# Two feed-forwards of a transformer kernel: their first chunk works on x without the root of the RMS norm, and its results are multiplied by the roots

## The chip, the cores and the metric

The kernel runs on one core of one Trainium2 chip, as one launch. The metric is the device time of that launch in microseconds (us). A core has a matrix engine (TensorE, PE in the profile), a vector engine (VectorE, DVE), a scalar engine (ScalarE, ACT), a general engine (GpSimd, POOL) and a queue for transfers (SyncE, SP). Each engine runs its own list of instructions in order; semaphores hold them together.

## The reference, cut to what matters

The reference is a model of two blocks of mixers, cross attentions and SwiGLU feed-forwards, and then a second part with a feed-forward of another kind. The change touches the two SwiGLU feed-forwards (l = 0 and 1) alone, each of which follows the output projection of a cross attention:

```python
def rms_norm(x, g, eps=NORM_EPS):
    xf = x.astype(jnp.float32)
    y = xf * lax.rsqrt(jnp.mean(xf * xf, axis=-1, keepdims=True) + eps)
    return (y * g.astype(jnp.float32)).astype(x.dtype)

def memory_cross_attention(h, mem, ..., wo):
    ...
    return out @ wo                       # 512 x 512 by 512 x 1024

def swiglu_ffn(h, norm, w13, w2):         # h 512 x 1024, hidden 2816
    u = rms_norm(h, norm) @ w13
    return (jax.nn.silu(u[..., :FFN_HIDDEN]) * u[..., FFN_HIDDEN:]) @ w2

h = h + memory_cross_attention(h, mem, ...)
h = h + swiglu_ffn(h, ffn_norm[i], ffn_w13[i], ffn_w2[i])
```

The root of a row (a token) is one number for all 1024 of its features, so (x * root * gain) @ W is (x * gain) @ W times that root, column by column of the tokens.

## The kernel before, in words

x lies transposed in SBUF: eight tiles `X[:, t, :]` of 128 features by 512 tokens. A product in nearly full float32 is made of three matmuls on float32r halves: weights high by x high, weights low by x high, weights high by x low (`Stream.tensor`). A `Stream` is a row of jobs, a job has chunks of up to 512 weight columns (four PSUM banks of 128 columns by 512 tokens), a chunk has one slice for each 128 features of the input. A slice is 12 matmuls for four banks. Chunks take the two sets of four banks in turn.

What each engine has to do for slices: ACT copies the weights of a slice to the high half (`round_slice`, L383), POOL subtracts to get the low half (`rest_of_slice`, L387), and there are four slots, so ACT's copy of slice s + 4 waits until PE is through slice s. All other work of ACT and DVE is written as generators, one for each finished chunk. `Stream.walk` puts them in a list and takes two steps of the first one in the list behind each slice (`rate` 2); on ACT these steps stand between the weight copies. DVE has no weight copies, so its instructions are simply the generators one after another, in the order of the chunks. A finish with `flush = 0` has ACT and DVE write out all that is pending at its first slice.

Around the change the stream of `cross_attention` has these jobs: `xo` (four slices in each of three chunks of 512, 256 and 256 columns; it adds to x), `up0` (six chunks of eight slices), `down0`, `up1`, `down1`.

- `AddToX.vector` (L853) adds each bank of `xo` to x. `AddToX.scalar` squares each tile of x (L628), `Rms.fold` (L635) adds up the squares of tiles 0 to 5 on DVE. `AddToX.tensor_end` stands at the end of `xo` in PE's list: a sum over the partitions of the folded squares and of tiles 6 and 7 (L649), idle matmuls that keep PE busy (`keep_busy`, L219), `spread_roots` (L657), and idle matmuls again.
- `Rms.roots` makes the mean (L695), ACT the square root (L663), DVE the inverse root (L2161 to L2169). `spread_roots` puts the roots in a PSUM bank, the same 512 in each partition. `Rms.scale` (L711) multiplies x by gain and by that bank, `Rms.round` (ACT, L669) makes the high half, `Rms.rest` (DVE, L678) the low half. PE waits for both in `up0`'s first chunk (`Finish.ready`, `ready_low`).
- `Gated` is the finish of `up0`: ACT takes the sigmoid of banks 0 and 1 (L1840), DVE multiplies by the same banks (L1852) and by banks 2 and 3 (L1857), ACT and DVE make the halves of the result (L1845, L1861).
- `Rider` is work of the second part that rides along: with each chunk of `up0`, DVE makes a sum over eight tiles of 128 by 512 (`Rider.vector`, one L905 and seven L910), behind the gated products of the chunk in DVE's list. In chunk c + 1, behind the slice t = 5, PE's list has `Gated.multiply(c)`: it waits for `made` of chunk c and, in `Rider.multiply`, for the rider's `summed` (four transposes, L930). `Rider.scalar` stands in ACT's list behind the gated work of the chunk; it waits for `first_used` and `summed` before it issues the next loads.

Of the kernel before, what the change touches and what calls it, by code (L numbers as in the profile page):

```python
# [286 lines left out]
class Stream:  # L287
# [53 lines left out]
    def tensor(self, pe):  # L341
        k = self.k
        for part in self.opening:
            part.tensor(pe)
        k.keep_busy(pe, 7, self.idle_first)
        for s, (q, job, c, t, finish, hi, lo) in enumerate(self.slices):
            if s >= self.opened:
                pe.wait_ge(self.rounded, s - self.opened + 1)
            finish.ready(pe, c, t)
            if t == 0 and q >= 2:  # L350
# [3 lines left out]
            for i, (w, a) in enumerate(((whi, hi(t)), (wlo, hi(t)), (whi, lo(t)))):  # L354
# [121 lines left out]
class Finish:  # L476

    flush, rate, after = None, 2, None  # L480

    def of(self, stream, job):
        self.stream, self.job = stream, job

    def signals(self, st):
        self.freed = st.signals(1)

    def ready(self, pe, c, t):

        if self.after and c == 0:  # L490
            self.after.await_high(pe, t)

    def ready_low(self, pe, c, t):
        if self.after and c == 0:
            self.after.await_half(pe, t)
# [85 lines left out]
class Rms:  # L581
# [122 lines left out]

    def scale(self, dve):

        for t in range(self.T + 1):
            if t < self.T:
                if self.split and t >= self.n_tmp:
                    dve.wait_ge(self.halved, self.tiles(t - self.n_tmp + 1))  # L710
                dve.scalar_tensor_tensor(out=self.tmp(t % self.n_tmp), in0=self.src(t), scalar=self.gain(t), in1=self.rows,  # L711
                                         op0=ALU.mult, op1=ALU.mult).then_inc(self.scaled, 1)
            if t >= 1 and self.split:
# [6 lines left out]
    def await_half(self, eng, t):  # L720
        eng.wait_ge(self.halved, self.tiles(t + 1))


# [58 lines left out]
class AddToX(Finish):  # L782
# [7 lines left out]
    def __init__(self, k, rms=None, gate=None, after=None, flush=None, ahead=None, rider=None, rms_later=False):  # L790
        self.folded = rms.T if rms_later else self.FOLDED
        if rms:
# [12 lines left out]
    def await_free(self, eng, c):  # L805
        eng.wait_ge(self.added, self.first(c + 1))
        if self.rms and not self.rms_later and c == len(self.job.widths) - 1:
            eng.wait_ge(self.rms.scaled, self.rms.T)
        if self.rider and c == 0:
# [12 lines left out]
    def tensor_end(self, pe):  # L822
        if self.rms_later:
            self.rms.sums_bank = self.sums_bank()
        elif self.rms:
            q2 = self.stream.first_chunk(self.job) + 2
# [21 lines left out]
    def vector(self, dve, link, q, c):  # L848
        for j in range(self.job.tiles(c)):
# [7 lines left out]
            ins.then_inc(self.added, 1)  # L857
            yield
        if self.rms:
            for t in range(max(self.first(c), 1), min(self.first(c + 1), self.folded)):  # L860
# [934 lines left out]
class Gated(Finish):  # L1795
# [8 lines left out]
    def signals(self, st):  # L1804
        self.bent, self.gated, self.made, self.rounded, self.halved = st.signals(5)
        if self.rider0 == 0:
            self.rider.signals(st)
# [17 lines left out]

    def tensor(self, pe, c, t):
        if c >= 1 and t == self.job.KT - 3:
            self.multiply(pe, c - 1)
# [6 lines left out]
    def scalar(self, act, q, c):  # L1835
        for p in range(2):
            self.stream.await_tile(act, q, p)
# [10 lines left out]

    def vector(self, dve, link, q, c):
        for p in range(2):  # L1850
# [7 lines left out]
        yield  # L1858
        for p in range(2):
            dve.wait_ge(self.rounded, 2 * c + p + 1)  # L1860
# [82 lines left out]
class Mixed(Finish):  # L1943
# [6 lines left out]
    def signals(self, st):  # L1950
        self.begun, self.tapped, self.bent, self.made = st.signals(4)

    def tensor_end(self, pe):
# [8 lines left out]
    def scalar(self, act, q, c):  # L1962
        for j in range(4):
            n = 4 * c + j
            self.stream.await_tile(act, q, j)
            at = self.tile0 + n
            act.activation(self.xbc[:, at, :], self.stream.bank(q, j), ACT.Identity, bias=col(self.k, "ssm_conv_b", at),  # L1967
                           scale=col(self.k, "ssm_conv_w3", at)).then_inc(self.begun, 1)
# [11 lines left out]

    def vector(self, dve, link, q, c):
        for lag in range(1, 4):
            for j in range(4):
                n = 4 * c + j
                if lag == 1:
                    dve.wait_ge(self.begun, n + 1)
                at = self.tile0 + n
                v = self.xbc[:, at, lag:S]
                ins = dve.scalar_tensor_tensor(out=v, in0=self.stream.bank(q, j)[:, 0:S - lag],  # L1989
                                               scalar=col(self.k, f"ssm_conv_w{3 - lag}", at), in1=v, op0=ALU.mult,  # L1990
# [751 lines left out]
def cross_attention(k, plan, l, name, out_halves, opening, squares_at, rows_at, spare_at, halves_at, mem_at, mem_halves_at,  # L2742
# [29 lines left out]

    rms = x_norm(k, lambda t: col(k, f"ffn_norm{l}", t), split_tiles(k, A_WORK, A_H), at=HID_AT + 8 * S)
    if l == 0:
# [32 lines left out]

def x_norm(k, gain, halves, shift=None, at=SCRATCH_AT, dst=None, n_squares=4):

# [3 lines left out]
    else:  # L2813
        tmp, n_tmp = (lambda i: dst[:, i, :]), DT
    return Rms(k, DT, lambda t: k.X[:, t, :], gain, halves, at, n_squares, at + n_squares * S, tmp, n_tmp, D, shift=shift)

# [1991 lines left out]
```

## Time and profile before

| | |
|---|---|
| median of 3 runs | 3426.64 us (3426.32 to 3426.74) |
| the profiled execution | 3427.0 us, its span 3425.3 us |
| PE busy | 3339.0 us, 97% of the span |
| DVE, ACT, POOL busy | 52%, 42%, 43% |
| mean granted clock of PE | 0.996 of full speed |

The trace gives for each instruction its engine, its line, start and duration. A matmul's duration is longer than its share of PE's time, since matmuls are pipelined; the pace is read from the distance of starts, or from the time and count of a long row. The two places of the change are at 545 us (l = 0) and at 1454 us (l = 1).

### The profile page before, as it was taken

What the parts mean: (1) busy time and instruction counts of PE and PEld (TensorE: products, weight loads), DVE (VectorE), ACT (ScalarE), POOL (GpSimd) and SP (SyncE); (2) the same over time, 40 slices, a digit from 0 to 9 for tenths busy, and PEclk for the clock granted to TensorE, in tenths of its full rate; (3) what the DMA queues carried; (4) which work ended last, traced back from release to release, by engine and by line L of the source; (5) the groups of instructions that cost most, each with busy time, mean ns of one, the idle gap of its engine ahead of it and who ended that gap; (6) DMA issues with size and microseconds to landing.
All of it is one profiled execution on the core that took longest, in us unless ns stands there. A gap on an engine that the chain in (4) does not pass through costs nothing. (4 is left out here: it accounts for less than half of the span.)

```text
span 3425.3 us, 48805 instructions
## 1 busy us (share of the span) xinstructions
PE 3339.0 (97%) x19319; PEld 2750.9 (80%) x19319; DVE 1781.4 (52%) x3104; ACT 1431.0 (42%) x2870; POOL 1483.4 (43%) x1337
## 2 busy tenths in 40 slices
PE   8999999999999999999999999999999999999999
PEld 7768778888877687888888877888888877888887
DVE  4665574636457674665363286445153176545243
ACT  4562354323344554532323246344343245444343
POOL 3330154454443545444544434445544433445543
PEclk9999999999999999999999999999999999999999
DMA  4210024545221022345443220222323220123321
GB/s 117 79 51 8 27 87 136 197 148 169 98 92 50 28 96 87 111 136 183 160 148 107 88 68 20 74 87 92 105 83 102 84 82 30 50 86 99 99 93 56
DMA packets 232830, 317.83 MB, mean 93 GB/s; under 512 B 9909, under 2 KB 149148, under 8 KB 232604
## 3 DMA queue, kind: packets, MB, share of 16 engines
q1 hardware_dynamic: 203206, 261.55, 23.8%
q10 hardware_dynamic: 29398, 53.17, 4.6%
q8 instruction: 154, 2.52, 0.3%
q14 instruction: 72, 0.59, 0.1%
HBM read 312.59 MB, written 2.10 MB: 92 GB/s over the span
## 5 line engine op out<-in xcount | busy, mean ns | idle before, releaser
L364 PE MATMUL banks<-split,split 128*128 128x512 f32 (+2 forms) x11760 | 2684.2, 389 | 27.7 <-ACT split L383 13.6
L364 PEld LDWEIGHTS banks<-split,split 128*128 128x128 f32 x11760 | 2186.9, 188 | 501.4 <-ACT split L383 24.4
L387 POOL TENSOR_TENSOR split<-kept,split 128x512 fp32r<-128x512 f32 (+2 forms) x1158 | 1356.4, 1176 | 1617.6 <-ACT split L383 1615.0
L383 ACT ACTIVATE split<-kept 128x512 fp32r<-128x512 f32 (+2 forms) x1158 | 646.1, 564 | 1460.1 <-PE banks L364 1416.8
L1913 DVE SCALAR_TENSOR_TENSOR work<-banks,kept,work 128x511 f32<-128x511 f32 (+1 forms) x176 | 120.4, 745 | 257.1 <-ACT work L1895 256.3
L910 DVE SCALAR_TENSOR_TENSOR work<-work,kept 128x512 f32<-128x512 f32 x168 | 195.5, 1164 | 6.0
L855 DVE SCALAR_TENSOR_TENSOR kept<-banks,kept 128x512 f32<-128x512 f32 x48 | 33.3, 745 | 209.6 <-PE banks L364 209.6
L853 DVE TENSOR_TENSOR kept<-banks,kept 128x512 f32<-128x512 f32 x64 | 40.5, 684 | 195.0 <-PE banks L364 195.0
L540 DVE COPY work<-banks 128x512 f32<-128x512 f32 (+1 forms) x64 | 37.4, 643 | 195.2 <-PE banks L364 195.2
L1852 DVE TENSOR_TENSOR work<-work,banks 128x512 f32<-128x512 f32 x44 | 28.3, 684 | 165.7 <-ACT work L1840 165.7
L1539 ACT ACTIVATE work<-work 128x128 f32<-128x128 f32 (+3 forms) x160 | 89.5, 560 | 48.4 <-DVE work L1599 47.6
L219 PE MATMUL banks<-kept 128*128 128x128 f32 x538 | 68.1, 277 | 10.7 <-PEq L246 10.7
L1989 DVE SCALAR_TENSOR_TENSOR work<-banks,kept,work 128x511 f32<-128x511 f32 (+2 forms) x72 | 49.1, 744 | 55.4 <-ACT work L1967 54.9
L219 PEld LDWEIGHTS banks<-kept 128*128 128x128 f32 x538 | 63.6, 192 | 13.7 <-issue 13.5
L1466 PE MATMUL banks<-kept,work 128*128 128x128 f32 x400 | 71.3, 276 | 0.6 <-ACT work L1539 0.6
L1599 DVE CUSTOM_DVE_ANT_0 work<-banks,kept 128x128 f32<-128x128 f32 (+3 forms) x96 | 46.8, 488 | 41.7 <-PE banks L1754 21.1
L635 DVE TENSOR_TENSOR work<-work 128x512 f32<-128x512 f32 x66 | 61.9, 938 | 5.4 <-DVE work L635 0.5
L1482 PE MATMUL banks<-work 128*64 128x128 f32 x592 | 61.3, 284 | 0.8 <-DVE work L1610 0.5
L669 ACT ACTIVATE split<-work 128x512 fp32r<-128x512 f32 x61 | 38.1, 630 | 56.0 <-DVE work L711 42.6
L1466 PEld LDWEIGHTS banks<-kept,work 128*128 128x128 f32 x400 | 48.8, 141 | 15.0 <-issue 6.2
L1895 ACT ACTIVATE work<-banks,kept 128x512 f32<-128x512 f32 x88 | 60.9, 771 | 0.0
L3693 PE MATMUL banks<-kept 64*64 64x64 f32 (+1 forms) x1408 | 55.4, 233 | 1.9 <-DVE kept L3928 1.4
(445 smaller groups left out, 3172.5 us busy)
## 6 DMA issues: line engine op xcount, KB each, us to landing
work<-in_mod_w ACTq DMA_DIRECT2D x48, 1024.0 KB, 5.9
kept<-in_ffn_w SPq DMA_DIRECT2D x94, 512.0 KB, 4.8
kept<-in_w_up SPq DMA_DIRECT2D x88, 512.0 KB, 4.5
kept<-in_w_in SPq DMA_DIRECT2D x36, 1024.0 KB, 5.0
kept<-in_od_w_in SPq DMA_DIRECT2D x20, 1024.0 KB, 5.0
kept<-in_ffn_w SPq DMA_DIRECT2D x18, 1024.0 KB, 5.2
kept<-in_w_down SPq DMA_DIRECT2D x18, 1024.0 KB, 5.0
kept<-in_ev_w_in SPq DMA_DIRECT2D x8, 1024.0 KB, 5.2
```

The lines of the kernel that those rows point to most:

```text
L219: pe.matmul(self.PS[:, bank, 0:P], self.ident, self.ones, start=True, stop=True)
L364: m = pe.matmul(self.bank(q, j), lhs, rhs, start=t == 0 and i == 0, stop=t == job.KT - 1 and i == 2)
L383: act.activation(self.weights(s, 0), self.source(s), ACT.Copy).then_inc(self.rounded, 1)
L387: pool.tensor_tensor(self.weights(s, 1), self.source(s), self.weights(s, 0), ALU.subtract).then_inc(self.k.slices_split, 1)
L635: dve.tensor_tensor(total, total, self.square_at(t), ALU.add).then_inc(self.folded, 1)
L910: ins = dve.scalar_tensor_tensor(out=self.sum, in0=self.slot[:, t, :], scalar=self.x[:, t:t + 1], in1=self.sum, op0=ALU.mult, op1=ALU.add)
L1466: m = pe.transpose(self.bank(self.TB[u % 2])[:, c * P:(c + 1) * P], self.prob[u % 4][:, c * P:(c + 1) * P], self.k.ident)
L1482: ins = pe.matmul(self.o_bank(h // 2)[i * 64:i * 64 + 64, t * P:(t + 1) * P], self.heads[h + i].v(c), self.probT[(u + i) % 3][:, c * P:(c ...
L1539: act.activation(tile, tile, ACT.Exp, bias=self.top[:, u % 8:u % 8 + 1], scale=-1.0, accum_out=self.total[:, u % 16:u % 16 + 1]).then_inc( ...
L1895: act.activation(self.cv[:, j, :], self.stream.bank(q, j), ACT.Identity, bias=col(self.k, f"conv_b_2{self.l}", at), scale=col(self.k, f"co ...
L1913: return dve.scalar_tensor_tensor(out=v, in0=self.stream.bank(q, j)[:, 0:S - lag], scalar=col(self.k, f"conv_w_2{self.l}{2 - lag}", self.c ...
L3693: m = pe.matmul(PS[half, bank, q * P:q * P + n], lhs(q)[half], rhs(q)[half], start=start, stop=stop)
```

## The change

For the norm in front of the two feed-forwards the class `Rms` gives way to `RmsBeside`.

- In `xo`, each tile of x gets its halves of x times gain, without the root, as soon as it is added: ACT makes the high half behind the square (`first_round`), DVE the low half behind the adds of the chunk (`first_rest`). All eight squares are folded on DVE (six before).
- `tensor_end` of `xo` issues nothing. `up0`'s first chunk takes the new halves (`await_first_high`, `await_first_half`), and no longer flushes. The sum stands behind its slice 2 (`SUM`), `spread_roots` behind its slice 4 (`SPREAD`), without idle matmuls.
- ACT's `root_of` stands behind the weight copy that waits for slice 3, and ACT copies the spread roots from PSUM to SBUF (`factors`, signal `kept`) behind the copy that waits for slice 5.
- `scale`, `round` and `rest` make the normed halves for chunks 1 to 5 in the same place as the first halves; `round` waits until PE is through the slice of chunk 0. `scale` reads the roots from SBUF (`factors`). On ACT these steps come two behind each weight copy.
- The first chunk's results take more steps on DVE (`first_products`): banks 0 and 1 times `factors`, times the sigmoid, times banks 2 and 3, times `factors`. They stand behind `scale` and `rest` in DVE's list, and in front of the rider's first sum.

```diff
 class Gated:
     def tensor(self, pe, c, t):
+        if self.early and c == 0:
+            self.early.beside(pe, t)
         if c >= 1 and t == self.job.KT - 3:
             self.multiply(pe, c - 1)
...
     def scalar(self, act, q, c):
         for p in range(2):
+            if self.early and c == 0:
+                act.wait_ge(self.first_made, p + 1)
+                act.activation(self.slot(1, p), self.slot(0, p), ACT.Sigmoid).then_inc(self.bent, 1)
+                continue
             self.stream.await_tile(act, q, p)
             if c >= 2:
                 act.wait_ge(self.halved, 2 * (c - 2) + p + 1)
+            elif self.early:
+                act.wait_ge(self.gated, p + 1)
...
+    def first_products(self, dve, q):
+        factors = self.early.factors
+        dve.wait_ge(self.early.kept, 1)
+        for p in range(2):
+            self.stream.await_tile(dve, q, p)
+            dve.tensor_tensor(self.slot(0, p), self.stream.bank(q, p), factors, ALU.mult).then_inc(self.first_made, 1)
+        yield
+        for p in range(2):
+            dve.wait_ge(self.bent, p + 1)
+            dve.tensor_tensor(self.slot(0, p), self.slot(0, p), self.slot(1, p), ALU.mult).then_inc(self.gated, 1)
+        yield
+        for p in range(2):
+            self.stream.await_tile(dve, q, 2 + p)
+            dve.wait_ge(self.gated, p + 1)
+            dve.tensor_tensor(self.slot(0, p), self.slot(0, p), self.stream.bank(q, 2 + p), ALU.mult).then_inc(self.second_made, 1)
+        yield
+        for p in range(2):
+            dve.wait_ge(self.second_made, p + 1)
+            dve.tensor_tensor(self.slot(0, p), self.slot(0, p), factors, ALU.mult).then_inc(self.made, 1)
+        yield
...
+class RmsBeside(Rms):
+
+    SUM, SPREAD = 2, 4
...
+    @property
+    def factors(self):
+        return self.sq[:, 3, :]
+
+    def first_round(self, act, t):
+        act.activation(self.first_halves(t)[0], self.src(t), ACT.Identity, scale=self.gain(t)).then_inc(self.first_rounded, 1)
+
+    def first_rest(self, dve, t):
+        dve.wait_ge(self.first_rounded, t + 1)
+        high, low = self.first_halves(t)
+        dve.scalar_tensor_tensor(out=low, in0=self.src(t), scalar=self.gain(t), in1=high, op0=ALU.mult,
+                                 op1=ALU.subtract).then_inc(self.first_halved, 1)
...
+    def beside(self, pe, t):
+        if t == self.SUM:
+            self.sum_folded(pe, self.k.PS[:, self.bank0 + 2, :])
+        if t == self.SPREAD:
+            self.spread_roots(pe, self.k.PS[:, self.bank0 + 3, :])
+
+    def finish_scalar(self, act, steps=1):
+        for _ in range(2 * self.SUM + 2):
+            yield
+        self.root_of(act)
+        for _ in range(2 * (self.SPREAD - self.SUM)):
+            yield
+        act.wait_ge(self.spread, 1)
+        act.activation(self.factors, self.rows, ACT.Copy).then_inc(self.kept, 1)
+        yield
+        for t in range(self.T):
+            if not self.first:
+                self.stream.await_slice(act, self.slice0 + t)
+            self.round(act, t)
+            yield
+
+
+    def finish_vector(self, dve, link):
+        self.roots(dve, link)
+        yield
+        dve.wait_ge(self.kept, 1)
+        yield from self.scale(dve, self.factors, self.first)
...
 class AddToX(Finish):
@@ scalar
                 self.rms.square(act, self.first(c) + j)
+            if self.beside:
+                self.rms.first_round(act, self.first(c) + j)
             yield
@@ vector
+        if self.beside:
+            for j in range(self.job.tiles(c)):
+                self.rms.first_rest(dve, self.first(c) + j)
+                yield
         if self.rms:
             for t in range(max(self.first(c), 1), min(self.first(c + 1), self.folded)):
                 self.rms.fold(dve, t)
@@ ffn_jobs
-    up0 = Gated(k, *hid, SG_AT, rider, 0, after=rms, flush=0)
+    up0 = Gated(k, *hid, SG_AT, rider, 0)
+    up0.early = rms
```

## Rows read from the trace of the kernel before

**Rows 1.** The page: span, busy time, the granted clock in 40 slices

```profile
span 3425.3 us, 48805 instructions
PE 3339.0 (97%) x19319; PEld 2750.9 (80%) x19319; DVE 1781.4 (52%) x3104; ACT 1431.0 (42%) x2870; POOL 1483.4 (43%) x1337
```

**Rows 2.** Timeline, l = 0: start us, us, engine, line, operation [idle before <-releaser]

```profile
544.62 1.08 PEld L649 LDWEIGHTS banks<-kept,work 128*128 128x128 f32 x8
...
544.84 1.05 PE L649 MATMUL banks<-kept,work 128*128 128x128 f32 x8
...
546.79 1.28 ACT L663 ACT_TABLE_LOAD   x1
...
548.53 0.20 ACT L663 ACTIVATE work<-work 128x4 f32<-128x4 f32 x1 [0.46 <-DVE work L695]
...
549.59 1.16 PE L657 MATMUL banks<-kept,work 128*128 128x128 f32 x8
...
550.79 1.41 DVE L711 SCALAR_TENSOR_TENSOR work<-kept,banks 128x512 f32<-128x512 f32 x2 [1.25 <-PE banks L657]
...
552.27 29.81 PEld L364 LDWEIGHTS banks<-split,split 128*128 128x128 f32 x132
```

**Rows 3.** Timeline, l = 1: the same two ends

```profile
1454.14 1.08 PEld L649 LDWEIGHTS banks<-kept,work 128*128 128x128 f32 x8
...
1461.79 30.27 PEld L364 LDWEIGHTS banks<-split,split 128*128 128x128 f32 x134
```

**Rows 4.** Timeline, l = 0: the rider's first sum and PE's transposes behind it

```profile
580.75 1.52 DVE L905 TENSOR_SCALAR work<-work,kept 128x512 f32<-128x512 f32 x1
...
582.31 8.28 DVE L910 SCALAR_TENSOR_TENSOR work<-work,kept 128x512 f32<-128x512 f32 x7
...
590.71 0.42 PEld L930 LDWEIGHTS banks<-kept,work 128*128 128x128 f32 x4 [0.47 <-issue]
...
591.10 21.62 PEld L364 LDWEIGHTS banks<-split,split 128*128 128x128 f32 x96
```

**Rows 5.** Timeline, l = 0, in xo: adds, squares, weight copies

```profile
533.48 2.48 DVE L853 TENSOR_TENSOR kept<-banks,kept 128x512 f32<-128x512 f32 x4 [11.51 <-PE banks L364]
...
534.49 1.14 ACT L628 ACTIVATE work<-kept 128x512 f32<-128x512 f32 x2
...
535.88 2.97 DVE L635 TENSOR_TENSOR work<-work 128x512 f32<-128x512 f32 x3
...
539.38 1.29 DVE L853 TENSOR_TENSOR kept<-banks,kept 128x512 f32<-128x512 f32 x2 [0.52 <-PE banks L364]
...
541.23 0.62 ACT L383 ACTIVATE split<-kept 128x512 fp32r<-128x512 f32 x1
```

**Rows 6.** Timeline, l = 0: two weight copies behind two slices, one split on POOL

```profile
571.66 0.63 ACT L383 ACTIVATE split<-kept 128x512 fp32r<-128x512 f32 x1 [2.09 <-PE banks L364]
...
574.38 0.63 ACT L383 ACTIVATE split<-kept 128x512 fp32r<-128x512 f32 x1 [2.09 <-PE banks L364]
...
575.09 1.29 POOL L387 TENSOR_TENSOR split<-kept,split 128x512 fp32r<-128x512 f32 x1 [1.43 <-ACT split L383]
```

**Rows 7.** Groups of DVE with shapes, 545 to 592 us: busy us, mean ns | idle before

```profile
L711 DVE SCALAR_TENSOR_TENSOR work<-kept,banks 128x512 f32<-128x512 f32 x8 | 5.8, 742 | 1.3 <-PE banks L657 1.3
L678 DVE TENSOR_TENSOR split<-work,split 128x512 fp32r<-128x512 f32 x8 | 5.5, 686 | 0.1
...
L1852 DVE TENSOR_TENSOR work<-work,banks 128x512 f32<-128x512 f32 x2 | 1.3, 684 | 15.7 <-ACT work L1840 15.7
L1857 DVE TENSOR_TENSOR work<-work,banks 128x512 f32<-128x512 f32 x2 | 1.3, 678 | 0.0
```

**Rows 8.** L910 over the whole trace: shortest, median, longest ns

```profile
L910 DVE SCALAR_TENSOR_TENSOR work<-work,kept x168: 750/753/1860, 582.3 to 1786.4; 128x512 f32<-128x512 f32 x168
```

**Rows 9.** Groups of DVE with shapes, 552 to 1000 us

```profile
L910 DVE SCALAR_TENSOR_TENSOR work<-work,kept 128x512 f32<-128x512 f32 x84 | 97.8, 1164 | 3.0
L1861 DVE TENSOR_TENSOR split<-work,split 128x512 fp32r<-128x512 f32 x22 | 21.0, 992 | 3.5 <-ACT split L1845 3.4
```

**Rows 10.** Timeline of PE: two restarts after long waits

```profile
138.49 11.21 PE L364 MATMUL banks<-split,split 128*128 128x512 f32 x36 [5.76 <-ACT split L383]
...
978.88 13.34 PE L364 MATMUL banks<-split,split 128*32 128x512 f32 x47 [4.64 <-ACT split L383]
```

**Rows 11.** Stretches: PE, PEld, DVE, ACT, POOL busy (x), granted clock, DMA share, GB/s

```profile
552.20:574.20 22.00, 22.00 (x100) 18.21 (x100) 8.95 (x14) 8.53 (x15) 8.91 (x7) 1.00 0.16 48
...
974.00:979.00 5.00, 0.36 (x3) 0.12 (x1) 4.96 (x8) 2.81 (x6) 0.10 (x1) 0.83 0.00 0
979.00:985.00 6.00, 6.00 (x16) 4.27 (x17) 5.93 (x7) 2.02 (x4) 5.87 (x5) 0.58 0.54 178
```

More of the change, by code:

```diff
@@ L349, in tensor @@
             finish.ready(pe, c, t)
+            high, low = finish.early.first_halves(t) if finish.early and c == 0 else (hi(t), lo(t))
             if t == 0 and q >= 2:
@@ L353, in tensor @@
             n = job.tiles(c)
-            for i, (w, a) in enumerate(((whi, hi(t)), (wlo, hi(t)), (whi, lo(t)))):
+            for i, (w, a) in enumerate(((whi, high), (wlo, high), (whi, low))):
                 if i == 1:
@@ L476 @@
 class Finish:
-    flush, rate, after = None, 2, None
+    flush, rate, after, early = None, 2, None, None
     def of(self, stream, job):
         self.stream, self.job = stream, job
+        if self.early:
+            self.early.follow_with(stream, job)
     def signals(self, st):
@@ L703, in finish_vector, with scale @@
         yield from self.scale(dve)
-    def scale(self, dve):
+    def scale(self, dve, rows=None, first=None):
+        rows = self.rows if rows is None else rows
         for t in range(self.T + 1):
@@ L710, in scale @@
                     dve.wait_ge(self.halved, self.tiles(t - self.n_tmp + 1))
-                dve.scalar_tensor_tensor(out=self.tmp(t % self.n_tmp), in0=self.src(t), scalar=self.gain(t), in1=self.rows,
-                                         op0=ALU.mult, op1=ALU.mult).then_inc(self.scaled, 1)
+                if first:
+                    self.stream.await_slice(dve, self.slice0 + t)
+                dve.scalar_tensor_tensor(out=self.tmp(t % self.n_tmp), in0=self.src(t), scalar=self.gain(t), in1=rows, op0=ALU.mult,
+                                         op1=ALU.mult).then_inc(self.scaled, 1)
             if t >= 1 and self.split:
@@ L721, in await_half, with first_halves, signals, follow_with @@
         eng.wait_ge(self.halved, self.tiles(t + 1))
+class RmsBeside(Rms):
+    SUM, SPREAD = 2, 4
+    first = None
+    def first_halves(self, t):
+        hi, lo = self.first or (self.hi, self.lo)
+        return hi(t), lo(t)
+    def signals(self, st):
+        super().signals(st)
+        self.first_rounded, self.first_halved, self.kept = st.signals(3)
+    def follow_with(self, stream, job):
+        self.stream = stream
+        self.slice0 = next(s for s, piece in enumerate(stream.slices) if piece[1] is job)
+        self.bank0 = (stream.first_chunk(job) - 1) % 2 * 4
+    @property
[8 more added lines that the diff above has]
+                                 op1=ALU.subtract).then_inc(self.first_halved, 1)
+    def await_first_high(self, eng, t):
+        eng.wait_ge(self.first_rounded, t + 1)
+    def await_first_half(self, eng, t):
+        eng.wait_ge(self.first_halved, t + 1)
+    def beside(self, pe, t):
[22 more added lines that the diff above has]
+        yield from self.scale(dve, self.factors, self.first)
 class RowsLater(Rms):
@@ L807, in await_free @@
         if self.rms and not self.rms_later and c == len(self.job.widths) - 1:
-            eng.wait_ge(self.rms.scaled, self.rms.T)
+            if self.beside:
+                eng.wait_ge(self.rms.kept, 1)
+            else:
+                eng.wait_ge(self.rms.scaled, self.rms.T)
         if self.rider and c == 0:
@@ L824, in tensor_end @@
             self.rms.sums_bank = self.sums_bank()
-        elif self.rms:
+        elif self.rms and not self.beside:
             q2 = self.stream.first_chunk(self.job) + 2
@@ L1826, in tensor @@
     def tensor(self, pe, c, t):
+        if self.early and c == 0:
+            self.early.beside(pe, t)
         if c >= 1 and t == self.job.KT - 3:
@@ L1858, in vector @@
         yield
+    def vector(self, dve, link, q, c):
+        yield from self.first_products(dve, q) if self.early and c == 0 else self.products(dve, q, c)
         for p in range(2):
@@ L1951, in signals, with tensor, raw @@
         self.begun, self.tapped, self.bent, self.made = st.signals(4)
+        if self.early:
+            self.first_made = st.signals(1)
+    def tensor(self, pe, c, t):
+        if self.early and c == 0:
+            self.early.beside(pe, t)
+    def raw(self, q, c, j):
+        return self.sg[:, j, :] if self.early and c == 0 else self.stream.bank(q, j)
     def tensor_end(self, pe):
@@ L1981, in vector @@
     def vector(self, dve, link, q, c):
+        if self.early and c == 0:
+            dve.wait_ge(self.early.kept, 1)
+            for j in range(4):
+                self.stream.await_tile(dve, q, j)
+                dve.tensor_tensor(self.raw(q, c, j), self.stream.bank(q, j), self.early.factors, ALU.mult).then_inc(
+                    self.first_made, 1)
+                if j % 2:
+                    yield
         for lag in range(1, 4):
```

34 lines of the change are left out of this document (24 added, 10 removed).

## The prediction

> **What bounds the kernel now.** Read first the busy line of the page: PE works 97% of the span [rows 1]. So a change can only win by taking waits or idle matmuls out of PE's list, and anything that makes PE wait is paid in full, unless PE waits further on for something that goes on meanwhile. Then the timeline at the change-over from `xo` to `up0`. PE's sum (L649) begins at 544.62, the first slice of `up0` at 552.27: 7.65 us in which PE does 3 us of sums and spreading and otherwise idle matmuls [rows 2]. At l = 1 it is again 7.65 us [rows 3]. These two stretches, 15.3 us or 0.45% of the span, are all that the change can win.
>
> Last, one looks for the next place behind the change where PE meets work of the engines that the change loads. It is the rider. Its first sum ends at 582.31 + 8.28 = 590.59, and PE's transposes, which wait for it, begin at 590.71, after 0.47 us without work [rows 4]. So PE and DVE arrive there together, 8 + 6 slices behind the start of `up0`: 552.27 to 590.24, or 2.71 us a slice; the distance of ACT's copies says the same, 574.38 - 571.66 = 2.72 [rows 6]. The cover of that sum is used up already.
>
> **The change part by part**, in times of l = 0.
>
> *When up0 starts.* ACT gets a high half of about 0.6 us behind each square, DVE a low half of about 0.75 (the shortest L910, which has the same two inputs in SBUF [rows 8]) behind each add. The adds of chunk 0 end at 535.96; ACT's squares begin at 534.49 [rows 5]. ACT has eight steps of 0.6 us and a weight copy between, so its fourth high half is there at 539.7. DVE's fourth low half is then done at 540.4, its three folds, 2.97 us before the change [rows 5], at 543.1 (I take 2.7, between that and three times the 0.75 above), and the adds of tiles 4 and 5, so far at 539.38 [rows 5], come at 543.1 to 544.4. ACT waits for them with squares and high halves, 4 x 0.6 us, and only then stands the copy of `up0`'s first weights, so far at 541.23 [rows 5]. It ends at 546.9. PE starts there, not at 544.6: of the 7.65 us, 5.4 are won. Bounds: 544.7 if all this hides, 548.5 if each DVE operation takes the mean of the stretch with POOL at work, 1.16 and 0.99 us [rows 9]. A further 0.4 us go as PE waits for POOL's first low half (1.29 us [rows 6], against 0.9 us for the four matmuls in front).
>
> *What stands inline.* The sum costs PE 1.05 us and spreading 1.16 [rows 2]. PE is through slice 2 at 546.9 + 0.4 + 3 x 2.71 = 555.4, through slice 3 at 555.4 + 1.05 + 2.71 = 559.2, through slice 4 at 561.9. The root is late by 0.4: ACT's copy behind slice 3 ends at 559.9, the table load takes 1.28 (so far it lay under the sum), the root 0.2, and from the root's start to the spreading it is 549.59 - 548.53 = 1.06 [rows 2]: 562.3. So PE is ready for the transposes at 546.9 + 0.4 + 1.05 + 0.4 + 1.16 + 37.97 = 587.9, which is 2.3 us earlier than the 590.24 of before.
>
> *When the rider's sum is there.* ACT copies the roots behind the copy that waits for slice 5: PE leaves that slice at 561.9 + 0.4 + 1.16 + 2.71 = 566.1 (rounded up), the copies take 0.65 and 0.6, `kept` is at 567.4. Before, `scale` began at 550.79 [rows 2]. DVE's list is one row, and in it stand, ahead of the rider: eight `scale` and eight `rest`, 8 x (0.75 + 0.68) = 11.4 us [rows 7, 8]; the first products, 2 x 0.64 (PSUM input; the shares of L1852's busy time [rows 7]); about 0.6 of waiting for the sigmoid; 2 x 0.68; 2 x 0.64; 2 x 0.68; 0.6 until ACT has rounded; low halves, 0.8 beyond that. That is 7.3. The rider itself, without POOL, takes some 5.9 (seven L910 of 0.75 with 0.03 between them, and 0.4 to 0.5 for the L905, which took 1.52 with a split beside it [rows 4, 8]). Without POOL the sum is thus at 567.4 + 11.4 + 7.3 + 5.9 = 592.0.
>
> POOL is not away. The seven L910 took 8.28 us where seven of the shortest take 5.3, and three splits of POOL lay beside them [rows 4, 8]: 1.0 us for each split. The products with a PSUM input keep their 0.68 beside a split [rows 7]. `scale` read the roots from PSUM and ran while POOL stood still, 0.74 us [rows 7]; now both inputs are in SBUF, and it runs while POOL splits slices. Five splits fall beside the 16 operations (+5), three beside the rider (+3, since ACT was held at `scaled` and `made`, and lets its copies go in a row then): 592.0 + 8 = 600.0. PE goes on with slices at 600.0 + 0.5 = 600.5, where it did at 591.10: +9.4 us. The whole start is won and lost again. Bounds: 587.9 for the sum (start at 544.7, so `kept` at 565.2; 10.1 for the pairs, which is 1.26 us a tile, the least that their overlap leaves; no split in the way; 0.6 less of waiting); 604.8 (start at 548.5, every SBUF operation at its mean of [rows 9], so 17.2 for the pairs and 8.8 for products and halves, the rider 590.59 - 580.75 = 9.8). I take 600.0, as the count of splits follows from the order of the lists.
>
> The Trainium skill bears on this term (SBUF — State Buffer, the section on its two separate sides): a VectorE operation with two SBUF inputs and a GpSimd operation that reads SBUF exclude each other for a whole instruction. By this rule moving the roots from PSUM to SBUF puts `scale` under POOL's splits. By L711's row alone, 0.74 with POOL idle, the five splits would cost `scale` and `rest` about 3 us less, and the sum would be at some 597. The rider's rows speak for the rule.
>
> *PE's clock.* PE stands from 587.9 to 600.1, about 12 us, and the idle matmuls that other places use are not there. After 5.76 and 4.64 us of waiting, 36 and 47 matmuls took 11.21 and 13.34 us [rows 10]; at 2.72 / 12 = 0.227 us each they would take 8.2 and 10.7: 3.0 and 2.6 us lost. The stretch behind such a wait shows a granted clock of 0.58, a mix of 1.2 and 2.4 GHz, where `up0` has 1.00 [rows 11]. I take 2.8. For the wait of 2 us in front of `up0`, less than half of either, I count nothing. Bounds: 0, and 3.4 for a wait that is twice as long as those of the rows.
>
> *Behind it.* Nothing gives it back: PE is busy through `up0` [rows 11], and each next rider sum starts from a finished chunk, so it moves with PE. ACT and POOL have all four slots filled when PE resumes.
>
> *Sum.* 9.4 + 2.8 = 12.2 us at each place, 24.4 for two. Against the profiled execution 3427.0 + 24.4 = 3451.4; the median is 0.4 lower than that execution: 3451.0. Least: 588.4 against 591.1 where PE goes on, -2.7 each, 3421.2. Most: 605.3 - 591.1 + 3.4 = 17.6 each, 3461.8.
>
> **The rivals.** A measurement of this kernel can tell about 0.2%, 6.9 us, from no change.
>
> - *DVE is done in time, the change does what it is shaped for.* Then PE resumes at 587.9 + 0.4 = 588.3, 2.8 us earlier than before: 3421.0, and if the start hides wholly, 5 us each, 3416.6. It decides at 23.2 us of DVE work between `kept` and 590.6. Against it: 24.6 us of work without any POOL. For it: 22.7 if the pairs take 1.26 us each. Faster by over 0.2% needs 3.4 us at each place, so start and DVE both at their best. 0.03, and 0.05 for the band within 0.2%, where DVE is at its best alone.
> - *The wait, but no drop of the clock:* 18.8 us, 3445.4. 0.08.
> - *A short wait:* POOL takes less, or the splits fall beside PSUM products; the sum is at 593 to 596, a wait of 5 to 8 us; +3 to +5.5 and some clock: 3433 to 3443. 0.12.
> - *Worse:* ACT, held at `scaled` and `made`, also starves PE of weights, as its copies stand behind the roundings; 3458 to 3463. 0.12.
>
> **How the numbers follow.** The forecast, 3451.0 with about 5 us to each side, has 0.60. Slower by over 0.2%: 0.60 + 0.08 + 0.12 + 0.12 = 0.92; within: 0.05; faster: 0.03. The range goes from 3438, which leaves out half of the short wait and the cases that win, to 3463, just over the upper bound.
>
> **What the profile after would show.** At each change-over PE's first `up0` matmul some 2 us behind the last of `xo` (right: start at 546 to 548.5); one L649 group and one L657 group inside the first chunk, the latter after a wait under 1 us; L711 with a mean over 1 us, not 0.74; the first L905 near 593, not 580.75; before the first transposes a wait of PE of about 12 us put down to DVE, and matmuls at a lower granted clock behind it. I am wrong if PE meets the transposes with no wait, or if the DVE chain from `kept` to `summed` takes under 25 us; also if PE waits for weights earlier than that.

## The result and the profile after

The changed kernel takes 3451.77 us (median of 6 runs, 3450.4 to 3452.58) where the kernel before takes 3426.5 (6 runs). The ratio is 1.0073, 95% interval 1.006 to 1.0086: slower by 25 us. The profiled execution has a span of 3450.1 us, 24.8 more than before.

The page's first lines, to be laid beside [rows 1]:

```profile
span 3450.1 us, 48701 instructions
PE 3334.6 (97%) x19223; PEld 2743.4 (80%) x19223; DVE 1813.3 (53%) x3132; ACT 1440.2 (42%) x2888; POOL 1491.6 (43%) x1337
```

PE has 96 matmuls and 4 us of busy time less: 64 idle matmuls are gone and, as all squares are now folded on DVE, 32 of the sum over the partitions. The span is longer all the same, so PE now waits. The waits of PE from 540 to 700 us (who waited for whom: us in total, times, longest); before the change this view was empty there:

```profile
PE banks L1019 <- DVE work L999: 11.0, 2, 9.9
PE banks L365 <- ACT split L384: 2.2, 1, 2.2
PE banks L660 <- DVE work L646: 1.9, 1, 1.9
PE banks L668 <- DVE work L2312: 0.3, 1, 0.3
PE banks L365 <- POOL split L388: 0.2, 1, 0.2
```

L1019 is the rider's transposes (L930 before), L999 the rider's sum (L910), L660 the sum of squares over partitions, L668 the spreading, L365 the slices. The timeline of the changed kernel at l = 0, to be laid beside [rows 2] and [rows 4]:

```profile
544.80 0.63 ACT L639 ACTIVATE work<-kept 128x512 f32<-128x512 f32 x1 [3.94 <-DVE kept L938]
...
547.09 2.17 ACT L384 ACTIVATE split<-kept 128x512 fp32r<-128x512 f32 x4
...
547.75 1.20 PE L365 MATMUL banks<-split,split 128*128 128x512 f32 x4 [2.23 <-ACT split L384]
...
558.58 1.16 PE L660 MATMUL banks<-kept,work 128*128 128x128 f32 x8 [1.88 <-DVE work L646]
...
565.55 1.16 PE L668 MATMUL banks<-kept,work 128*128 128x128 f32 x8 [0.32 <-DVE work L2312]
...
570.64 2.07 DVE L724 SCALAR_TENSOR_TENSOR work<-kept,work 128x512 f32<-128x512 f32 x2 [5.14 <-ACT work L787]
...
585.82 1.27 DVE L1953 TENSOR_TENSOR work<-banks,work 128x512 f32<-128x512 f32 x2
...
592.20 1.50 DVE L994 TENSOR_SCALAR work<-work,kept 128x512 f32<-128x512 f32 x1
...
593.74 7.24 DVE L999 SCALAR_TENSOR_TENSOR work<-work,kept 128x512 f32<-128x512 f32 x7
...
601.12 1.08 PE L1019 MATMUL banks<-kept,work 128*128 128x128 f32 x4 [9.91 <-DVE work L999]
...
601.86 23.68 PE L365 MATMUL banks<-split,split 128*128 128x512 f32 x96
...
626.65 0.63 PE L1019 MATMUL banks<-kept,work 128*128 128x128 f32 x4 [1.12 <-DVE work L999]
...
648.93 0.60 PE L1019 MATMUL banks<-kept,work 128*128 128x128 f32 x4
```

`up0` starts at 547.75 and not at 552.27. DVE's list then runs from `scale` at 570.64 without a gap of note to the end of the rider's sum at 600.98, and PE stands 9.9 us in front of the transposes. Behind them 96 matmuls take 23.68 us.

To compare kernels place by place I use one stretch: from the start of the first four adds of `xo` to the third group of transposes. Before it goes from 533.48 [rows 5] to this row, 101.8 us:

```profile
635.23 0.60 PE L930 MATMUL banks<-kept,work 128*128 128x128 f32 x4
```

In the changed kernel it goes from 534.00 to 648.93, 114.9 us; at l = 1 it is 114.4 against 101.8. That is 13.2 and 12.6 us. Ahead of the first place the two profiles differ by +0.5, between the places by +0.1, behind the second by -1.6; together 24.8, the difference of the spans. Behind the second place all kernels here have the same instructions, and their profiles still differ there by up to 4.3 us (1878.9 in this one, 1883.2 in e4_no_split), so effects of a few us are read from the stretch.

### The profile page after: what moved, and what is told of

It reads as the page before. It is cut to its first block and busy times, and to the rows that moved or that the text cites. A ratio compares the mean times of both kernels' runs of the same rounds, so it can differ in the third digit from the quotient of the medians.

```text
span 3450.1 us, 48701 instructions
## 1 busy us (share of the span) xinstructions
PE 3334.6 (97%) x19223; PEld 2743.4 (80%) x19223; DVE 1813.3 (53%) x3132; ACT 1440.2 (42%) x2888; POOL 1491.6 (43%) x1337
## 5 line engine op out<-in xcount | busy, mean ns | idle before, releaser
L365 PE MATMUL banks<-split,split 128*128 128x512 f32 (+2 forms) x11760 | 2689.2, 389 | 32.6 <-ACT split L384 18.1
L365 PEld LDWEIGHTS banks<-split,split 128*128 128x128 f32 x11760 | 2188.7, 188 | 508.6 <-ACT split L384 29.8
L999 DVE SCALAR_TENSOR_TENSOR work<-work,kept 128x512 f32<-128x512 f32 x168 | 193.1, 1149 | 6.0
L646 DVE TENSOR_TENSOR work<-work 128x512 f32<-128x512 f32 x70 | 73.7, 1053 | 5.4 <-DVE work L646 0.5
L219 PE MATMUL banks<-kept 128*128 128x128 f32 x474 | 60.0, 277 | 10.7 <-PEq L246 10.7
L219 PEld LDWEIGHTS banks<-kept 128*128 128x128 f32 x474 | 56.0, 192 | 13.7 <-issue 13.5
L639 ACT ACTIVATE work<-kept 128x512 f32<-128x512 f32 x88 | 52.8, 623 | 21.1 <-DVE kept L938 14.3
```

The costliest lines, as they stand in the source:

```text
L219: pe.matmul(self.PS[:, bank, 0:P], self.ident, self.ones, start=True, stop=True)
L639: act.activation(self.square_at(t), self.src(t), ACT.Square).then_inc(self.squared, 1)
L646: dve.tensor_tensor(total, total, self.square_at(t), ALU.add).then_inc(self.folded, 1)
L999: ins = dve.scalar_tensor_tensor(out=self.sum, in0=self.slot[:, t, :], scalar=self.x[:, t:t + 1], in1=self.sum, op0=ALU.mult, op1=ALU.add)
```

## The experiments

All nine kernels are edits of the changed one, and all times stand against runs of the kernel before on the same chip. The stretch is that of l = 0 / l = 1. Line numbers shift from kernel to kernel: the transposes of the rider are L1019 in the changed kernel and L1020 to L1047 in the others.

| kernel | median us | ratio to before (95%) | stretch us | wait at first transposes |
|---|---|---|---|---|
| changed | 3451.8 | 1.0073 (1.006 to 1.0086) | 114.9 / 114.4 | 9.9 |
| e1_no_rider_sum | 3445.5 | 1.0057 (1.0042 to 1.0072) | 111.6 / 110.9 | 6.3 |
| e2_meet_later | 3449.7 | 1.0067 (1.0052 to 1.0082) | 112.5 / 112.6 | 6.3 |
| e3_keep_busy | 3452.1 | 1.0074 (1.0059 to 1.0089) | 112.9 / 112.9 | 1.4 behind the idle matmuls |
| e4_no_split | 3443.0 | 1.0047 (1.003 to 1.0063) | 108.2 / 109.4 | 3.5 |
| e5_rider_first | 3429.8 | 1.0007 (0.9997 to 1.0016) | 102.8 / 102.9 | none |
| e7_start_only | 3442.1 | 1.0044 (1.003 to 1.0058) | 110.6 / 110.5 | 9.9 |
| e6_rider_and_start | 3426.9 | 0.9997 (0.9987 to 1.0006) | 101.6 / 101.7 | none |
| e8_rider_start_steps | 3422.0 | 0.9987 (0.9978 to 0.9996) | 98.8 / 100.4 | none |
| e9_two_and_six | 3418.3 | 0.9972 (0.9962 to 0.9982) | 97.1 / 97.1 | 0.4 |

**Is it DVE's list, with the rider's sum last in it?** The first kernel shortens that sum.

```diff
+                n = 8 if i == 0 else 512
-                ins = dve.scalar_tensor_tensor(out=self.sum, in0=self.slot[:, t, :], ...
+                ins = dve.scalar_tensor_tensor(out=self.sum[:, 0:n], in0=self.slot[:, t, 0:n], ...
```

> The changed kernel, but the first rider sum adds only 8 of its 512 columns in seven of its eight operations (the rest of that sum is left out). Theory (PE waits at the transposes for DVE's list, the rider's sum last in it): the seven L999 shrink from 7.2 to some 1.6 us, the sum comes at about 595.4 instead of 601.0, PE's wait there falls from 9.9 to about 4.3 us at each place, 3451.8 - 2 x 5.6 = 3440.6; if the shorter wait also spares part of the clock's drop, down to 3437. Rival (the loss sits in the start of the chunk and in what stands inline on PE, and the wait would only be filled by something else): PE waits nearly as long, 3449 to 3452.

Its timeline at the same place:

```profile
591.79 3.89 POOL L388 TENSOR_TENSOR split<-kept,split 128x512 fp32r<-128x512 f32 x3 [2.50 <-ACT split L384]
...
593.37 3.63 DVE L1000 SCALAR_TENSOR_TENSOR work<-work,kept 128x8 f32<-128x8 f32 x7
...
597.15 1.09 PE L1020 MATMUL banks<-kept,work 128*128 128x128 f32 x4 [6.33 <-DVE work L1000]
597.89 23.92 PE L365 MATMUL banks<-split,split 128*128 128x512 f32 x96
```

DVE's seven operations lose 3.6 us (7.24 to 3.63), PE's wait 3.6 us (9.91 to 6.33), the stretch 3.4 and 3.5. So each microsecond off DVE's list is one off PE's wait, as the theory has it, and the rival falls. My size was wrong: I gave the seven operations 1.6 us. Taken one by one, from narrower windows of the same timeline, they show why:

```profile
593.37 1.10 DVE L1000 SCALAR_TENSOR_TENSOR work<-work,kept 128x8 f32<-128x8 f32 x1
...
595.73 0.23 DVE L1000 SCALAR_TENSOR_TENSOR work<-work,kept 128x8 f32<-128x8 f32 x1
```

The first took 1.10 us, the second, at 594.51, 1.18, both beside POOL's three splits, which end at 595.68; the five behind them took 0.23 each and follow each other in 0.26. So a small operation that meets a split is held up too, which bears on the question of POOL below. The shorter wait spared nothing of the clock's cost. The total fell by 6.3 us, the two stretches by 6.9.

**Can PE do something in the meantime?**

```diff
-        if c >= 1 and t == self.job.KT - 3:
+        if c >= 1 and t == self.job.KT - (1 if self.early and c == 1 else 3):
             self.multiply(pe, c - 1)
```

> The changed kernel, but PE meets the first rider sum behind slice 7 of the second chunk instead of slice 5. Theory: two more slices, 5.4 us, fit before the wait, which falls from 9.9 to 4.5 us, up to 6 if POOL's splits for them fall beside the rider; but the next chunk then waits for the rider's result, about 1.4 us. Net 2.5 to 4 us at each place: 3444 to 3447, and 2 us less at each if the clock stays up. Rival (PE has no work ready behind slice 5, since ACT's weight copies are held too): no gain, 3450 to 3453.

```profile
593.19 9.07 DVE L999 SCALAR_TENSOR_TENSOR work<-work,kept 128x512 f32<-128x512 f32 x7
...
602.40 1.09 PE L1019 MATMUL banks<-kept,work 128*128 128x128 f32 x4 [6.34 <-DVE work L999]
604.57 17.98 PE L365 MATMUL banks<-split,split 128*128 128x512 f32 x72 [1.07 <-DVE kept L1013]
```

The two slices do fit in, so the rival falls. Of their 5.4 us, the wait gives back 3.6: the seven L999 now take 9.07 instead of 7.24, with PE and so POOL going on beside them. And the next chunk waits 1.07 us for the rider's result. The stretch gains 2.4 and 1.8, a little less than I gave it. The total, 3449.7, fell by 2.1 us alone and lies above the 3444 to 3447 that I expected: the profile of this kernel is 2.1 us longer outside the two stretches.

**What does the clock cost?**

```diff
     def multiply(self, pe, c):
         q = self.stream.first_chunk(self.job) + c
         pe.wait_ge(self.made, 2 * c + 2)
+        if self.early and c == 0:
+            self.k.keep_busy(pe, q % 2 * 4 + 1, 38)
         self.rider.multiply(pe, self.rider0 + c, self.k.PS[:, q % 2 * 4, :])
```

> The changed kernel with 38 idle matmuls (some 9.3 us) on PE between its wait for the gated products and its wait for the first rider sum. Theory (the long wait lets the granted clock fall, and the matmuls behind it pay some 2 us at each place): granted clock 1.00 behind the wait, 96 matmuls there in 22.1 us and not 23.7 and 23.1, 3451.8 - 4 = 3448. Rival (the clock costs nothing that is not hidden by the next wait): 3451 to 3453.

```profile
592.20 8.66 PE L219 MATMUL banks<-kept 128*128 128x128 f32 x76
602.22 0.65 PE L1019 MATMUL banks<-kept,work 128*128 128x128 f32 x4 [1.36 <-DVE work L999]
602.63 22.04 PE L365 MATMUL banks<-split,split 128*128 128x512 f32 x96
```

At the place itself the theory holds: 22.04 us for the 96 matmuls instead of 23.68 (and of 23.10 at l = 1), the stretch shorter by 2.0 and 1.5. The total doesn't show it: 3452.1, the rival's number. Outside the two stretches this profile is 4.9 us longer than that of the changed kernel (1.1 ahead of the first, 1.0 between them, 2.7 behind the second). Windows of the trace show one cause of it (PE, PEld, DVE, ACT, POOL busy, then the granted clock), in the changed kernel and then in this one:

```profile
1094.00:1098.00 4.00, 3.81 (x31) 3.43 (x32) 2.26 (x6) 2.41 (x5) 0.00 (x0) 1.00 0.00 0
```

```profile
1094.00:1098.00 4.00, 4.00 (x23) 3.91 (x22) 2.28 (x5) 2.35 (x5) 0.00 (x0) 0.57 0.02 4
```

In a mixer that neither kernel changes, the clock falls for some microseconds in one kernel and not in the other. Four microseconds at 0.57 instead of 1.00 are worth 1.7 us (an estimate from these two rows), and a gain of 3.5 us in all can't be told from a few of them. Whether such falls make up all of the 4.9 us is not shown. I take the clock's cost from the stretch alone.

**Does POOL slow DVE?** Here POOL splits only a strip of the slices that lie beside DVE's list; the rest of their low halves is left out.

```diff
+        if finish.early and 9 <= 8 * c + t < 18:
+            pool.tensor_tensor(self.weights(s, 1)[:, 0:8], self.source(s)[:, 0:8], self.weights(s, 0)[:, 0:8], ALU.subtract)...
```

> The changed kernel, but POOL splits only 8 of 512 columns of the weights of nine slices (slices 1 to 7 of the second chunk, 0 and 1 of the third); their other low halves are left out. Theory (DVE operations with two SBUF inputs stand still while POOL works): L724's mean goes from 1.21 to 0.75 us, L689's from 0.79 to 0.69, the seven L999 take some 5.5 instead of 7.2 us and the L994 0.5 instead of 1.5; the list is shorter by about 7 us, PE's wait at the transposes 2.5 to 3 us instead of 9.9, the clock stays up: 3451.8 - 2 x (7 + 2) = 3434. Rival (DVE is slowed by something else, ACT and PE reading the same memory or waits for ACT's roundings): the means stay above 1 us, 3449 to 3452.

Groups of DVE with shapes, 545 to 604 us (busy us, mean ns): the changed kernel, then this one, with L729, L694 and L1004 for L724, L689 and L999.

```profile
L724 DVE SCALAR_TENSOR_TENSOR work<-kept,work 128x512 f32<-128x512 f32 x8 | 9.6, 1214 | 5.1 <-ACT work L787 5.1
L999 DVE SCALAR_TENSOR_TENSOR work<-work,kept 128x512 f32<-128x512 f32 x7 | 7.0, 1003 | 0.2
...
L689 DVE TENSOR_TENSOR split<-work,split 128x512 fp32r<-128x512 f32 x8 | 6.3, 788 | 0.3 <-ACT split L680 0.2
```

```profile
L729 DVE SCALAR_TENSOR_TENSOR work<-kept,work 128x512 f32<-128x512 f32 x8 | 5.9, 746 | 5.2 <-ACT work L792 5.2
L694 DVE TENSOR_TENSOR split<-work,split 128x512 fp32r<-128x512 f32 x8 | 5.5, 690 | 1.0 <-ACT split L685 0.9
L1004 DVE SCALAR_TENSOR_TENSOR work<-work,kept 128x512 f32<-128x512 f32 x7 | 5.3, 752 | 0.2
```

```profile
594.01 0.88 PE L1024 MATMUL banks<-kept,work 128*128 128x128 f32 x4 [3.48 <-DVE work L1004]
594.54 23.51 PE L365 MATMUL banks<-split,split 128*128 128x512 f32 x96
```

Without the splits each of these operations takes its shortest time, and PE's wait is 6.4 us shorter. The rival falls. That is what the Trainium skill (SBUF — State Buffer, the section on its two separate sides) says of operations with two SBUF inputs, and this run agrees. The rider's first operation, which reads one tile and a scalar for each partition, is held up too: 1.50 us in the changed kernel, 0.48 here. The total came to 3443 and not 3434. One part of that is the clock, which did not stay up: a wait of 3.5 us cost as much behind it (23.51 here, 24.49 at l = 1, against 22.04) as one of 9.9. Another, 3.4 us, lies outside the two stretches and stays open; the stretches fell by 6.8 and 5.0.

**Is it the order?** The next kernel computes all, and takes the rider's sum to the front.

```diff
     def finish_vector(self, dve, link):
-        self.roots(dve, link)
+        dve.wait_ge(self.summed, (self.turn + 1) * self.n_sums)
+        sums = self.bank.rearrange("p (t n) -> p t n", n=P)[:, :, 0]
+        dve.tensor_scalar(self.mean, sums, 1.0 / self.dim, EPS, ALU.mult, ALU.add).then_inc(self.averaged, 1)
+        yield from self.rider.sum_up(dve, link, 0, 0, 4)
+        dve.wait_ge(self.rooted, self.turn + 1)
+        inverse_root(dve, link, self.mean, self.root, self.t, self.inverted)
         yield
+        yield from self.rider.sum_up(dve, link, 0, 4, DT)
         dve.wait_ge(self.kept, 1)
...
     def vector(self, dve, link, i, bank):
-        for t in range(DT):
+        if not (self.early and i == 0):
+            yield from self.sum_up(dve, link, i, 0, DT)
+        yield from self.take(dve, link, i, bank)
```

> The changed kernel with the first rider sum moved to the front of DVE's list: four of its operations between the mean and the inverse root, four between the inverse root and the copied roots, where DVE stands idle 4.8 and 5.1 us in the changed kernel. All is computed. Theory (the loss is the order in DVE's list): kept and scale stay where they are, PE meets the transposes with a wait under 1 us instead of 9.9, the clock stays up; the stretch from the first add of xo to the third group of transposes, 114.9 and 114.4 us (101.8 before), falls to about 103; total 3427 + 2 to 3 = 3429. Rival (DVE's work is too long in any order, the wait only moves to the gated products): the wait is still over 5 us, total over 3438.

```profile
590.36 0.60 PE L1034 MATMUL banks<-kept,work 128*128 128x128 f32 x4
...
613.88 0.63 PE L1034 MATMUL banks<-kept,work 128*128 128x128 f32 x4 [1.11 <-DVE work L1012]
```

The wait of 9.9 is gone, the stretch is 102.8 where about 103 was expected, the time 3429.8. With the same instructions in another order, nearly all of the loss goes. This kernel can't be told from the one before (interval 0.9997 to 1.0016). So the start that the change wins pays for what stands inline, and no more.

**And the start?** Here the rider stays last, and only the orders in and behind `xo` change.

```diff
     def scalar(self, act, q, c):
+        if self.beside and c == 1:
+            yield
+            yield
...
         if self.beside:
-            for j in range(self.job.tiles(c)):
-                self.rms.first_rest(dve, self.first(c) + j)
+            rests, folds = ((range(4), ()), ((), range(1, 6)), (range(4, 8), range(6, 8)))[c]
+            for t in folds:
+                self.rms.fold(dve, t)
                 yield
-        if self.rms:
+            for t in rests:
+                self.rms.first_rest(dve, t)
+                yield
+        elif self.rms:
```

> The changed kernel with only the start mended: ACT copies the first weights of up0 ahead of the squares of tiles 4 and 5, and DVE adds up squares before it makes low halves that are needed late (tiles 4 to 7); the rider's sum stays last. Theory (the waits of 2.2 us in front of up0 and 1.9 us in front of the sum come from these two orders, and all of DVE's list moves with them): both waits go, roots are kept 4 to 5 us earlier, PE's wait at the transposes stays at about 10 us, since PE and DVE gain alike; the stretch falls from 114.9 and 114.4 by 4 to 5, total 3452 - 9 = 3443. Rival (an earlier PE only waits longer at the same moment, as DVE's list does not move): total within 2 us of 3452.

Its waits of PE at l = 0, all of them:

```profile
PE banks L1026 <- DVE work L1006: 11.0, 2, 9.9
PE banks L668 <- DVE work L2319: 0.3, 1, 0.3
```

The waits of 2.2 and 1.9 us are gone. The stretch loses 4.4 and 3.9, the time 3442.1 was expected at 3443, and the wait at the transposes is still 9.9: mending the start takes nothing from the loss at the transposes. Both edits together:

> Both edits: the rider's first sum in front, and the start mended. Theory (the two losses are independent): the stretch falls to about 98.5 us against 101.8 before, total 3427 - 6.5 = 3420.5, faster than both kernels. Rival (the gated products of the first chunk are the next to come late, as PE is 4 us earlier): a wait of 3 to 5 us at the transposes, total 3427 to 3430.

```profile
PE banks L668 <- DVE work L2334: 2.7, 1, 2.7
PE banks L1041 <- DVE work L1019: 1.1, 1, 1.1
```

```profile
556.62 3.23 DVE L1019 SCALAR_TENSOR_TENSOR work<-work,kept 128x512 f32<-128x512 f32 x3
...
557.98 0.21 ACT L674 ACTIVATE work<-work 128x4 f32<-128x4 f32 x1
...
559.77 0.17 DVE L2326 RECIPROCAL work<-work 128x4 f32<-128x4 f32 x1
...
561.44 1.24 PE L668 MATMUL banks<-kept,work 128*128 128x128 f32 x8 [2.72 <-DVE work L2334]
```

The expectation missed by 3 us a place, and neither case named the cause: the total is the rival's, 3426.9, but there is no wait at the first transposes. The two gains don't add up. The gap in front of the root is no gap for four of the rider's operations: ACT has the root at 558.2, DVE comes to it at 559.8, and PE stands 2.7 us in front of the spreading, with a mean granted clock of 0.91 from 560 to 580. Two more edits follow. The expectation of the first was written before this kernel had run, and its total of 3418.5 starts from the 3420.5 said here. In it, ACT's steps for the rider behind the first chunk, 11 before, become 2:

```diff
     def scalar(self, act, i, last):
+        if self.early and i == 0:
+            for half in range(2):
+                act.wait_ge(self.summed if half else self.first_used, 1)
+                self.load(act, 1, half)
+                yield
+            return
```

> Both edits, and ACT's steps for the rider behind the first chunk cut from 11 to 2 (the two loads alone). Theory (the wait of 1.1 us at the second group of transposes comes from ACT's list, in which the first chunk's steps begin two slices late and push the sigmoid of the second chunk behind one more weight copy): that wait goes, the stretch is 1 us shorter than with both edits alone, total 3418.5. Rival (that wait comes from the rider's own length): unchanged to that kernel.

The wait of 1.1 us at the second transposes is gone:

```profile
610.98 0.60 PE L1047 MATMUL banks<-kept,work 128*128 128x128 f32 x4
```

It was ACT's list that made it. The stretch falls by more than this, 2.9 and 1.3; beyond the 1.1 it is the clock, which at l = 0 doesn't fall in this kernel. The total is 3422.0, 4.9 us under the kernel before it and 3.5 over what was said. Then the rider's sum is divided two and six:

```diff
-        yield from self.rider.sum_up(dve, link, 0, 0, 4)
+        yield from self.rider.sum_up(dve, link, 0, 0, 2)
...
-        yield from self.rider.sum_up(dve, link, 0, 4, DT)
+        yield from self.rider.sum_up(dve, link, 0, 2, DT)
```

> The kernel with both edits and the two rider steps on ACT, but only two operations of the rider's first sum stand in front of the inverse root, and six behind it. Theory (in the kernel with four and four, DVE is still in the rider when the root is there: the operations end at 559.9, the root at 558.2, and PE waits 2.7 us in front of the spreading): that wait falls to about 0.3 us, the roots are kept 2.4 us earlier, the stretch from the first add to the third group of transposes falls from 98.8 to about 96.4 us (101.8 before); where the shorter wait spares a drop of the clock, 1.7 us more at that place. Total 3427 - 2 x 5.4 = 3416. Rival (six operations are too long for the second gap, so scale begins late and the wait moves to the transposes): the stretch stays over 98 us, total 3420 or more.

```profile
561.29 6.65 DVE L1025 SCALAR_TENSOR_TENSOR work<-work,kept 128x512 f32<-128x512 f32 x6
...
561.43 1.16 PE L668 MATMUL banks<-kept,work 128*128 128x128 f32 x8 [0.39 <-DVE work L2340]
562.34 24.77 PE L365 MATMUL banks<-split,split 128*128 128x512 f32 x108
587.52 0.66 PE L1047 MATMUL banks<-kept,work 128*128 128x128 f32 x4 [0.40 <-DVE work L1994]
```

Two waits of 0.4 us are left. The stretch is 97.1 at both places, 4.7 us under that of before; twice that is 9.4, and the time is 9.2 us under the runs of before beside it (3418.26 against 3427.47). This version beats both kernels. I expected 96.4 and 3416.

## Why the prediction was right

The forecast was 3451.0, the time 3451.8. The forecast's own times are given for the kernel before; the changed kernel's trace runs 0.5 later from the start of `xo` on, which I take off here.

- *The mechanism.* PE and DVE met at the transposes with nothing to spare, and the change made DVE's list later while PE's grew shorter. Runs e1 and e5 show it, one by taking a part away, one by order alone.
- *Start of up0:* 546.9 said, 547.2 measured. The row of ACT shows the reason as foretold: the weight copies stand at 547.09 behind squares that waited 3.94 us for the adds.
- *Inline on PE:* the sum and the spreading cost 1.16 each, and the wait for the root 0.32 was said to be 0.4. Missed was a wait of 1.88 us in front of the sum (0.29 at l = 1). The step that failed is the folds. I priced the three of chunk 0, at 2.7 us (they took 3.52), and put the four behind them, on which the sum waits, at nothing; they took 1.68 each (the row below) where the three of before had taken 0.99. They too have two inputs in SBUF, and POOL splits one slice after another beside them (547.77 to 553.76 and from 554.97). I counted POOL's splits for `scale` and the rider and forgot them here. That it is the splits that stretch the folds is read from these rows; no run took those splits away.

```profile
L646 DVE TENSOR_TENSOR work<-work 128x512 f32<-128x512 f32 x4 | 6.7, 1682 | 0.2
```

- *kept:* 567.4 said, 570.1 measured, in the main from that wait and the late start.
- *DVE from there:* `scale` and `rest` 16.4 said, 15.2 measured (570.64 to 585.82); products and halves 7.3 and 6.4; the rider 8.9 and 8.8. So the chain was 30.3 us and not 32.6, and it began 2.7 later: the sum at 600.5 and not 600.0. Two errors of over 2 us cancelled: that is luck.
- *PE's wait* was 9.9, not 12, as PE was later too; PE went on 10.2 us later than before (601.86 less 0.5, against 591.10), not 9.4.
- *Clock:* 2.8 said. Measured 1.6 and 1.1 in the slices behind the wait (23.68 and 23.10 against 22.04 of e3), and 0.4 in the transposes (1.08 against 0.63 to 0.65). For the wait in front of `up0`, 2.23 us, I counted nothing. At l = 1 the clock did fall behind it, to 0.59 from 1472 to 1474 us, and 32 matmuls took 9.15 us where they took 7.53 at l = 0:

```profile
1471.93 9.15 PE L365 MATMUL banks<-split,split 128*128 128x512 f32 x32 [0.22 <-POOL split L388]
```

It cost nothing there only because PE had to wait for the folds in any case: the wait in front of the sum is 0.29 us at l = 1 and 1.88 at l = 0, and the sum begins 10.8 us behind the first slice at both.
- *Behind it nothing:* wrong by 1.1 us. ACT's steps for the first chunk began two slices late, and the second chunk's sigmoid slid behind one more weight copy. My reading of ACT's list stopped at the first transposes. e8 shows that the cause is ACT's list.
- *The rule of the Trainium skill* (SBUF — State Buffer, the section on its two separate sides) on two SBUF inputs weighed 3 us of the forecast; e4 bears it out, with 6.4 us in all.

The sum of 12.2 us a place was measured as 13.2 and 12.6. The two stretches make 25.8 us, 24.4 was said. That the spans differ by 24.8 alone comes from the 1.6 us by which the profile is shorter behind the second place, which no term of the forecast says; that too is luck. Of the rivals, the one on the faster side failed where it was said to: DVE's work from `kept` took 30 us and would have had to take 23. What tells between the kernels is the order on DVE, which no rival had as its own case: with it, the start and ACT's steps mended, the shape of the change does win.

## What to carry to other kernels

Before work is moved beside a stretch, look past it for the next place where the bounding engine meets the engine that gets the work, and read the slack there: here there was none, as the sum ended at 590.59 and the transposes began at 590.71. In a list that runs in order, work for a nearer meeting goes ahead of work for a farther one, and small gaps (4.8 and 5.1 us here) hold it if it is cut to their size. A step that is moved to where another engine is at work must be priced with that engine beside it.

## What was not expected of the hardware

- The clock's cost doesn't follow the length of the wait. Behind waits of 9.9, 6.3 and 3.5 us (changed kernel, e1, e4) the 96 matmuls took 23.68, 23.92 and 23.51 us at l = 0, and 23.10, 23.26 and 24.49 at l = 1, against 22.04 at the full clock. Behind a wait of 2.7 us the mean granted clock from 560 to 580 us is 0.91 in e6 and 1.00 in e8; waits of 0.4 (e9) leave 22.05.
- Short falls of the granted clock come and go elsewhere in kernels that are the same there (0.57 against 1.00 at 1094 to 1098 us), so single effects under some 3 us have to be read from a stretch of the trace.
- A DVE operation on 8 columns takes 0.23 us by itself and 1.10 and 1.18 us beside POOL's splits of 1.3 us (e1). They lose some 0.9 us each, and an operation on 512 columns about 1.0 (1.80 against 0.74, L724): what a split cost DVE here hardly depended on the size of the operation beside it.
